# Moving tokens' rows to and from the experts by indirect transfers in place of products with zeros and ones

## The chip, the cores and the metric

The kernel runs on one core of one Trainium2 chip; the chip's other cores run nothing. The metric is device time in microseconds (us) of one execution, from the run's own clock. The core has a TensorE (PE in the profile, its weight loads PEld), a VectorE (DVE), a ScalarE (ACT), a GpSimd (POOL) and a SyncE (SP), each with its own instruction stream, which meet by semaphores, and 16 DMA engines that serve transfers issued by SP and by POOL.

## The reference

Two networks follow one another over the same 256 tokens of width 1,024, in float32, batch 1. The part that changes is the mixture of experts in the first network's second layer:

```python
h = modulate(x, moe_norm, shift, scale)        # rmsnorm(x, w) * (1 + scale) + shift
logits = h @ router                            # 256 x 8
top_val, top_idx = lax.top_k(logits, 2)
weights = softmax(top_val)
gate_e = sum(one_hot(top_idx, 8) * weights)    # 256 x 8, two of eight not zero
out = 0
for e in range(8):
    g, u = split(h @ w_gu[e], 2)               # 1024 x 7168
    out = out + gate_e[..., e] * ((silu(g) * u) @ w_down[e])   # 3584 x 1024
x = x + gate * out
```

Each token needs two of the eight experts. Everything before it (two hybrid and dense blocks, a Mamba-2 mixer) and behind it (the final norm, two more hybrid layers) stays as it is.

## The kernel before, in words

The program is a list of stages; `program` calls each stage's `sync`, `tensor`, `vector`, `scalar` and `gpsimd` in turn, so each engine has one fixed order of instructions. Tokens lie on the 128 partitions in two halves of 128 (`hf`). X holds the running sum, xn the normed tokens.

The stage `experts` routes first. `routed_tensor` and `routed_vector` compute the logits, for each token and expert whether it is among the two best (`sel`), and its place in that expert's list (`pos`, a running count by products with a triangular matrix). An expert takes up to CAP = 128 tokens in a round. If one has more, a flag makes every engine run a second round (`again`) for places 128 to 255; all engines read the flag at the end of the first round (`second`).

Then `round_tensor`, `round_scalar` and `round_vector` go through 8 experts x 42 units (`U`). A unit is half of a 2 MB weight tile: 28 units make the hidden rows (seven groups j; gate and up part p_; two halves of the contraction each), 14 units are the projection down. Products run as three float32r products (high by high, low by high, high by low), so each unit is first split: ScalarE copies its rounded part (`split_hi`, line 139), VectorE subtracts (`split_lo`, line 145), then PE multiplies (`use_tensor`, line 132, 12 products of 128x512). Units have three buffers, so the split of unit n waits until PE has used unit n - 3. ScalarE and VectorE run two units ahead of PE (`AHEAD`): in step n they split unit n and then do what belongs to unit n - 2 (`use_scalar`, `use_vector`): the silu and the product of the hidden rows, the split of the transposed hidden rows. SP streams the weight tiles in the order of use (`pieces`, line 177) into three places of 2 MB; a place comes free when VectorE has split its last unit. The weights are 21 tiles an expert.

How tokens come to an expert (`gather_*`): VectorE builds the table Pe of zeros and ones (128 tokens x 128 places for each half) out of pos and sel. PE transposes it (line 136; VectorE copies it to PT) and forms XG = xn' x Pe, which gives the expert's tokens already transposed: 8 column blocks x 2 halves, in two steps of 16 products. VectorE applies scale and shift, and the split follows into XGh and XGl. `coming` places these six steps behind units 29 to 34 of the expert before, one step a unit; for expert 0 they run inside the routing.

How results come back (`put_*`, `rounded_sum_scalar`, `low_sum_vector`): when expert x is done, VectorE multiplies its rows by the gate of the whole block (`summed_vector`, into Y); during the next expert's first eight units the rows are split into Yh and Yl, PE multiplies PT by both for each half of the tokens and of the columns (8 products of 128x512, behind unit 7), and VectorE adds ps x egate into X (line 153, four instructions). The last expert's put follows at the end of the round.

Before this stage, the `mamba` stage's `gpsimd` issues small loads, then two row loads of 512 KB (`row_load`, eb from ssm_sums), then waits for PE before each further one. In `experts`, `gpsimd` loads the router's weights and the final norm, and nothing more until the next stage.

Of the kernel before, what the change touches and what calls it, by code (L numbers as in the profile page):

```python
# [6 lines left out]
F32 = mybir.dt.float32  # L7
# [4 lines left out]
D = 1024  # L12
T = 256
# [10 lines left out]
NE = 8  # L24
BIG = 1e30
CAP = 128


def constants():

    p = np.arange(128)
    c = {}
    c["ident"] = np.eye(128)
    c["causal"] = p[:, None] <= p[None, :]
    c["glamask"] = (p[:, None] <= p[None, :]) & (p[:, None] // 64 == p[None, :] // 64)
    lev = np.zeros((128, 7, 128))
    for n in range(7):
        b = p >> n
        lev[:, n, :] = (b[None, :] % 2 == 1) & (b[:, None] == b[None, :] - 1)
    c["levels"] = lev.reshape(128, -1)  # L40
    dist = np.zeros((128, 256))
    dist[:, :128] = 128 + p[:, None] - p[None, :]
    dist[:, 128:] = np.where(p[:, None] >= p[None, :], p[:, None] - p[None, :], BIG)
    c["dist"] = dist
    dc = np.full((128, 2, 16), BIG)
    for h in range(2):
        t = h * 128 + p
        for n in range(15):
            dc[:, h, n] = np.where(n * 16 + 31 <= t, t - (n * 16 + 15.5), BIG)
    c["distc"] = dc.reshape(128, -1)  # L50
    c["blockdiag"] = (p[:, None] // 16 == np.arange(8)[None, :])
    c["cmask"] = np.where(p[:, None] >= p[None, :], 0.0, -BIG)
    half = 8
    inv = np.float32(500000.0) ** (-np.arange(half, dtype=np.float32) / np.float32(half))
    ang = np.arange(T, dtype=np.float32)[None, :] * inv.astype(np.float32)[:, None]
    cos, sin = np.ones((128, T)), np.zeros((128, T))
    perm = np.zeros((128, 128))
    for b in (0, 64):
        cos[b:b + 8] = cos[b + 8:b + 16] = np.cos(ang.astype(np.float32))
        sin[b:b + 8] = -np.sin(ang.astype(np.float32))  # L60
        sin[b + 8:b + 16] = np.sin(ang.astype(np.float32))
        for i in range(8):
            perm[b + 8 + i, b + i] = 1
            perm[b + i, b + 8 + i] = 1
    c["cos"], c["sin"], c["perm"] = cos, sin, perm
    e = np.arange(8)
    c["tie"] = np.broadcast_to((e[None, :] < e[:, None]).reshape(1, 64), (128, 64))
    c["iota"] = np.broadcast_to(np.arange(256)[None], (128, 256))
    c["before"] = p[:, None] < p[None, :]
    c["reset64"] = np.broadcast_to((np.arange(T) % 64 != 0)[None], (128, T))  # L70
    c["reset128"] = np.broadcast_to((np.arange(T) % 128 != 0)[None], (128, T))
    return {k: np.ascontiguousarray(v, dtype=np.float32) for k, v in c.items()}
# [42 lines left out]
DONE = Done()  # L115
# [3 lines left out]
class Engine:  # L119
# [56 lines left out]
    def dma_start(self, o, i):  # L176
        return self.e.dma_start(o, i) if self.e else DONE

# [1947 lines left out]
def mamba(c):  # L2126
# [40 lines left out]
    for i in range(16):  # L2167
# [3 lines left out]
        if i % 4 == 3:  # L2171
            k = i // 4
# [29 lines left out]
    sums = c.nc.dram_tensor("ssm_sums", (32, T), F32).ap()  # L2202
    sums_landed, row_landed = c.event_signal("ssm_sums_landed", 16), [c.event_signal(f"ssm_row{i}_landed", 16) for i in range(2)]
# [16 lines left out]
    def gpsimd(e):  # L2220
# [8 lines left out]
        for j in range(2):  # L2229
            row_load(e, j)  # L2230
        for j in range(8):
# [284 lines left out]
def experts(c):  # L2516
# [15 lines left out]
    fl, fli = c.sb("fl", [1, 2], ph), c.sb("fli", [1, 1], ph, mybir.dt.int32)  # L2532
    ph.close()
# [5 lines left out]
    Pe = c.put(68.5, "Pe", [128, 2, 128])  # L2539
    hrow = [c.put(70.5 + 2 * i, f"hrow{i}", [128, 512]) for i in range(2)]  # L2540
# [44 lines left out]

    def gather_tensor(e, S, blk, x, step):
        if step == 1:
# [6 lines left out]
        if step in (2, 3):  # L2594
            k0 = 4 * (step - 2)
            ps = ubanks.take((S.name, "XG", x, k0))
            e.wait_ge(*ps.was)
            e.wait_ge(*S.v.at(("Pe", x)))
# [5 lines left out]
    def gather_vector(e, S, blk, x, step):  # L2604
        if step == 0:
# [5 lines left out]
        if step == 2:  # L2611
            ps = c.psum.of((S.name, "PT", x))
            e.wait_ge(*S.t.at(("PT", x)))
            if x > 1:
                e.wait_ge(*S.t.at(("put", x - 2)))
# [82 lines left out]
    def use_tensor(e, S, W, n):  # L2698
        x, l = at(n)
        hi, lo = W.parts(e, n)  # L2700
        if l < 28:
# [14 lines left out]
            if l == 7 and x:  # L2716
                put_tensor(e, S, x - 1)
# [21 lines left out]
    def use_scalar(e, S, n):  # L2739
        x, l = at(n)  # L2740
        if l == 2 and x:
            rounded_sum_scalar(e, S, x - 1)
# [28 lines left out]
    def use_vector(e, S, n):  # L2771
        x, l = at(n)
        if l == 4 and x:
            low_sum_vector(e, S, x - 1)
        if l < 28:
# [9 lines left out]
            if l == 7 and x:  # L2785
                put_vector(e, S, x - 1)
            return
# [4 lines left out]

    def summed_vector(e, S, x):
        e.wait_ge(*c.side.v.at(("gate", "moe")))
        e.wait_ge(*(S.t.at(("put", x - 1)) if x else M.t.at("logits")))
# [71 lines left out]
    def routed_vector(e):  # L2867
# [21 lines left out]
        e.tensor_reduce(sel[:, :, :].rearrange("p h e -> p (h e)"), e3(p1), ALU.add).then_inc(*v.up())  # L2889
        e.wait_ge(*v.now())  # L2890
        e.tensor_scalar(sel[:, :, :], sel[:, :, :], 1.5, ALU.is_lt).then_inc(*v.up("sel"))
# [8 lines left out]
        e.tensor_scalar(fl[:, 1:2], fl[:, 0:1], CAP + 0.5, ALU.is_gt).then_inc(*v.up())  # L2900
        e.wait_ge(*v.now())
        e.tensor_copy(fli[:, :], fl[:, 1:2]).then_inc(*v.up("flag"))
        e.wait_ge(*M.a.at("L"))
# [6 lines left out]
        e.tensor_tensor(gt[:, :, :], gt[:, :, :], bc(e1_[:, :], 2, 8), ALU.mult).then_inc(*v.up("gate"))  # L2910

# [15 lines left out]
    def gpsimd(e):  # L2927
        before.wait_for(e, "end")
        e.dma_start(rw[:, :, :], io["moe_router"][0].rearrange("(k p) e -> p k e", p=128)).then_inc(*router_landed.up("router"))
        e.dma_start(fn[:, :], io["final_norm"].partition_broadcast(128)).then_inc(*norm_landed.up("norm"))  # L2930
        M.g.mark("end")
# [1145 lines left out]
```

## Time and profile before

| what | us |
|---|---|
| median of three runs | 2509.26 |
| lowest, highest | 2507.23, 2512.62 |
| the profiled execution's own time | 2510.2 |
| its span, first to last instruction | 2508.4 |

| engine | busy us | share of the span |
|---|---|---|
| PE | 2374.4 | 95% |
| PEld | 2078.2 | 83% |
| DVE | 1976.5 | 79% |
| ACT | 1460.8 | 58% |
| POOL | 219.3 | 9% |

Times in the profile count from the span's start. A row of a timeline has the start, the length, the engine, the line of the kernel, the operation and its tiles, and in brackets how long the engine was idle before it and what released it. The line is often that of a helper (132 is every product, 136 every transpose, 145 every two-operand VectorE instruction), so tiles tell the operations apart. An engine that is not on the chain of waits may idle at no cost, and a busy PE is not PE at its peak. A DMA share is the mean busy share of the 16 DMA engines.

### The profile page before, as it was taken

What the parts mean: (1) busy time and instruction counts of PE and PEld (TensorE: products, weight loads), DVE (VectorE), ACT (ScalarE), POOL (GpSimd) and SP (SyncE); (2) the same over time, 40 slices, a digit from 0 to 9 for tenths busy, and PEclk for the clock granted to TensorE, in tenths of its full rate; (3) what the DMA queues carried; (4) which work ended last, traced back from release to release, by engine and by line L of the source; (5) the groups of instructions that cost most, each with busy time, mean ns of one, the idle gap of its engine ahead of it and who ended that gap; (6) DMA issues with size and microseconds to landing.
All of it is one profiled execution on the core that took longest, in us unless ns stands there. A gap on an engine that the chain in (4) does not pass through costs nothing.

```text
span 2508.4 us, 33025 instructions
## 1 busy us (share of the span) xinstructions
PE 2374.4 (95%) x13939; PEld 2078.2 (83%) x13939; DVE 1976.5 (79%) x2135; ACT 1460.8 (58%) x1679; POOL 219.3 (9%) x271
## 2 busy tenths in 40 slices
PE   5898999899989999999999999998999999899998
PEld 4776998798878888888888888887888997887997
DVE  6857876699669989898989998986667865767875
ACT  3334433467557777677777777774555654445562
POOL 1100111101000000000000000001401211320110
PEclk9987998999989999999999999999999999999999
DMA  9753677444459999999999999985124554223551
GB/s 328 245 189 127 251 282 291 176 170 168 172 193 369 343 371 344 363 350 360 355 361 353 361 355 355 361 343 187 68 101 151 200 191 159 98 77 119 209 211 68
DMA packets 143031, 612.71 MB, mean 244 GB/s; under 512 B 18696, under 2 KB 33370, under 8 KB 121370
## 3 DMA queue, kind: packets, MB, share of 16 engines
q1 hardware_dynamic: 125968, 554.39, 59.7%
q0 software_dynamic: 15824, 55.72, 6.4%
q8 instruction: 111, 1.82, 0.3%
q10 hardware_dynamic: 1082, 0.40, 0.1%
q14 instruction: 46, 0.38, 0.0%
HBM read 609.40 MB, written 1.08 MB: 243 GB/s over the span
## 4 chain that ended last, share of the span: by engine, by line
PE 79%; DVE 12%; ACT 4%; DMA 3%; issue 2%; POOL 1%; SPq 0%; DVEq 0%; ACTq 0%; POOLq 0%
PE ps L132 76%; PE ps L136 3%; DVE macc L153 1%; DVE eb L145 1%; DVE gate L153 1%; DVE ul_ssm_w L145 1%; DMA beside<-in_moe_mod_w 1%; DMA slots<-in_hyb_mod_w 1%; ACT xn L139 1%; DMA beside<-in_dense_mod_w 1%; DVE xn L150 0%; DVE xn L153 0%; DVE ul_in L145 0%; POOL Ci L145 0%; DVE xn L145 0%
## 5 line engine op out<-in xcount | busy, mean ns | idle before, releaser
L145 DVE TENSOR_TENSOR ul_moe_w<-slots,uh_moe_w 128x2048 fp32r<-128x2048 f32 x334 | 761.5, 2289 | 90.4 <-ACT uh_moe_w L139 89.4
L139 ACT ACTIVATE uh_moe_w<-slots 128x2048 fp32r<-128x2048 f32 x334 | 640.0, 1917 | 199.8 <-PE ps L132 167.2
L132 PE MATMUL ps<-uh_moe_w,XGh 128*128 128x512 f32 x896 | 354.4, 396 | 3.1 <-DVE XGl L145 2.1
L132 PE MATMUL ps<-uh_moe_w,XGl 128*128 128x512 f32 x896 | 349.6, 390 | 0.0
L132 PE MATMUL ps<-ul_moe_w,XGh 128*128 128x512 f32 x896 | 349.0, 389 | 0.0
L145 DVE TENSOR_TENSOR ul_ffn<-slots,uh_ffn 128x2048 fp32r<-128x2048 f32 x64 | 145.8, 2291 | 79.3 <-ACT uh_ffn L139 79.3
L132 PE MATMUL ps<-HTf,uh_ffn 128*128 128x256 f32 x704 | 199.4, 283 | 2.0 <-DVE HTlf L145 2.0
L132 PEld LDWEIGHTS ps<-uh_moe_w,XGh 128*128 128x128 f32 x896 | 168.3, 188 | 39.8 <-DVE ul_moe_w L145 3.8
L132 PE MATMUL ps<-HTf,ul_ffn 128*128 128x256 f32 x704 | 199.2, 283 | 0.0
L132 PE MATMUL ps<-HTlf,uh_ffn 128*128 128x256 f32 x704 | 199.2, 283 | 0.0
L132 PEld LDWEIGHTS ps<-uh_moe_w,XGl 128*128 128x128 f32 x896 | 168.2, 188 | 35.9
L132 PEld LDWEIGHTS ps<-ul_moe_w,XGh 128*128 128x128 f32 x896 | 168.4, 188 | 33.3
L132 PE MATMUL ps<-uh_moe_w,ehTh 128*128 128x512 f32 x448 | 177.2, 396 | 0.0
L132 PE MATMUL ps<-ul_moe_w,ehTh 128*128 128x512 f32 x448 | 174.6, 390 | 0.0
L139 ACT ACTIVATE uh_ffn<-slots 128x2048 fp32r<-128x2048 f32 x66 | 125.4, 1910 | 72.4 <-PE ps L132 70.7
L132 PE MATMUL ps<-uh_moe_w,ehTl 128*128 128x512 f32 x448 | 138.1, 389 | 0.0
L132 PEld LDWEIGHTS ps<-HTf,uh_ffn 128*128 128x128 f32 x704 | 135.1, 192 | 2.4 <-DVE HTlf L145 2.4
L132 PEld LDWEIGHTS ps<-HTlf,uh_ffn 128*128 128x128 f32 x704 | 135.2, 192 | 0.0
L132 PEld LDWEIGHTS ps<-HTf,ul_ffn 128*128 128x128 f32 x704 | 135.2, 192 | 0.0
L139 ACT ACTIVATE uh_dense_w<-slots 128x2048 fp32r<-128x2048 f32 x33 | 62.9, 1911 | 83.3 <-PE ps L132 83.2
L132 PE MATMUL ps<-HTm,uh_in 128*128 128x256 f32 (+1 forms) x336 | 100.8, 300 | 4.2 <-DVE ul_in L145 3.0
L145 DVE TENSOR_TENSOR ul_dense_w<-slots,uh_dense_w 128x2048 fp32r<-128x2048 f32 x33 | 75.5, 2289 | 36.2 <-ACT uh_dense_w L139 36.0
(530 smaller groups left out, 5531.6 us busy)
## 6 DMA issues: line engine op xcount, KB each, us to landing
slots<-in_moe_w_gu SPq DMA_DIRECT2D x111, 2048.0 KB, 9.4
slots<-in_moe_w_down SPq DMA_DIRECT2D x56, 2048.0 KB, 9.0
slots<-in_w_up SPq DMA_DIRECT2D x20, 2048.0 KB, 8.0
slots<-in_w_in SPq DMA_DIRECT2D x14, 2048.0 KB, 8.7
slots<-in_dense_w_gu SPq DMA_DIRECT2D x10, 2048.0 KB, 11.1
slots<-in_ssm_w_in SPq DMA_DIRECT2D x10, 2048.0 KB, 8.4
slots<-in_w_down SPq DMA_DIRECT2D x10, 2048.0 KB, 8.3
slots<-in_dense_w_down SPq DMA_DIRECT2D x5, 2048.0 KB, 10.9
```

The source lines that it names most:

```text
L132: return self.e.matmul(o, lhsT, rhs, start=start, stop=stop, skip_group_check=skip) if self.e else DONE
L136: return self.e.transpose(o, i, ident[0:n, 0:n]) if self.e else DONE
L139: return self.e.activation(o, i, f, **kw) if self.e else DONE
L145: return self.e.tensor_tensor(o, a, b, op) if self.e else DONE
L153: return self.e.scalar_tensor_tensor(o, a, s, b, op0, op1) if self.e else DONE
```

## The change

Row numbers are worked out in the routing. `place` is a new constant (each expert's first row, and rows out of the way). For each token and each of its two choices, VectorE forms the row place + pos, or a row out of the way (from NOWHERE) if the place is over 127: `to`, and `fro`, the same but at most row 896. 15 small VectorE instructions do this, 12 ahead of the gates and three behind (`share`, the weights of the two choices).

Two tables in memory, `moe_sent` and `moe_made`, take rows of 4 KB. POOL zeroes those parts of them that may be read without having been written, in the mamba stage, by eight stores of 512 KB. After the routing, POOL scatters xn into `moe_sent` by four indirect transfers (two halves x two choices, 128 rows each). For experts 1 to 7 POOL loads the 128 rows of an expert into Xrow, and PE transposes them (eight transposes of 128x128) in place of the 16 products a step; expert 0 keeps its products. The results of experts 0 to 6 are stored from Y to `moe_made` in place of the put. During expert 7, four indirect transfers gather each token's two rows, and VectorE adds them to X, times their share, behind units 12, 14, 16 and 18. Expert 7 keeps its table and its put, and the second round keeps everything.

```diff
+NOWHERE = (NE + 2) * CAP
...
+    c["place"] = np.concatenate([np.tile(np.arange(NE) * CAP, (128, 2)), NOWHERE + p[:, None] + np.array([[0, 128]])], 1)
...
+    def scatter_rows(self, o, rows, i):
+        return self.e.indirect_dma_start(o, bass.IndirectOffsetOnAxis(ap=rows, axis=0), i, None) if self.e else DONE
+
+    def gather_rows(self, o, i, rows):
+        return self.e.indirect_dma_start(o, None, i, bass.IndirectOffsetOnAxis(ap=rows, axis=0)) if self.e else DONE
...
+    zero = c.put(41.5, "zero", [128, 256])
+    c.sent = c.nc.dram_tensor("moe_sent", (NOWHERE + T, D), F32).ap()
+    c.made = c.nc.dram_tensor("moe_made", (NE * CAP, D), F32).ap()
+    c.zeroed = c.event_signal("moe_rows_zeroed", 16)
...
         e.wait_ge(*sums_landed.at("sums"))
         for j in range(2):
             row_load(e, j)
+        e.memset(zero[:, :], 0.0).then_inc(*g.up("zero"))
+        e.wait_ge(*g.at("zero"))
+        for x in range(1, NE):
+            e.dma_start(c.sent[x * CAP:(x + 1) * CAP, :].rearrange("p (a n) -> p a n", n=256), bc(zero[:, :], 1, 4)).then_inc(*c.zeroed.up("zeroed"))
+        e.dma_start(c.made[(NE - 1) * CAP:NE * CAP, :].rearrange("p (a n) -> p a n", n=256), bc(zero[:, :], 1, 4)).then_inc(*c.zeroed.up("zeroed"))
         for j in range(8):
...
+    Xrow, Yrow = c.put(120, "Xrow", [128, D]), [HT[:, 0:4, :].rearrange("p a b -> p (a b)"), c.put(120, "Yrow1", [128, D]), c.put(102.5, "Yrow2", [128, D])]
...
+    def placed(S, x):
+
+        return S is again or x in (0, NE - 1)
...
     def gather_tensor(e, S, blk, x, step):
-        if step == 1:
+        if step == 1 and (S is again or x == NE - 1):
...
             e.wait_ge(*ps.was)
+            if S is M and x:
+                e.wait_ge(*xrow_landed.at(("xrow", x)))
+                for k in range(k0, k0 + 4):
+                    m = e.transpose(ps.t[:, (k - k0) * 128:(k - k0 + 1) * 128], Xrow[:, k * 128:(k + 1) * 128], K["ident"])
+                m.then_inc(*S.t.up(("XG", x, k0)))
+                return
...
-        if step == 0:
+        if step == 0 and placed(S, x):
...
-        if step == 2:
+        if step == 2 and (S is again or x == NE - 1):
             ps = c.psum.of((S.name, "PT", x))
             e.wait_ge(*S.t.at(("PT", x)))
-            if x > 1:
+            if x > 1 and S is again:
...
-            if l == 7 and x:
+            if l == 7 and x and S is again:
                 put_tensor(e, S, x - 1)
...
-        if l == 2 and x:
+        if l == 2 and x and S is again:
             rounded_sum_scalar(e, S, x - 1)
...
-        if l == 4 and x:
+        if l == 4 and x and S is again:
             low_sum_vector(e, S, x - 1)
...
-            if l == 7 and x:
+            if l == 7 and x and S is again:
                 put_vector(e, S, x - 1)
+            if S is M and x == NE - 1 and l in COMING_BACK:
+                come_back_vector(e, COMING_BACK.index(l))
...
+    COMING_BACK = (12, 14, 16, 18)
+
+    def come_back_vector(e, i):
+        o = X[:, i % 2, :]
+        e.wait_ge(*M.v.at("share"))
+        e.wait_ge(*yrow_landed[i % 3].at(("yrow", i)))
+        if i > 1:
+            e.wait_ge(*M.v.at(("back", i - 2)))
+        e.scalar_tensor_tensor(o, Yrow[i % 3][:, :] if i % 3 else Yrow[0], share[:, i:i + 1], o, ALU.mult, ALU.add).then_inc(*M.v.up(("back", i)))
+        if i == 3:
+            M.v.mark(("X", NE - 2))
+
     def summed_vector(e, S, x):
         e.wait_ge(*c.side.v.at(("gate", "moe")))
-        e.wait_ge(*(S.t.at(("put", x - 1)) if x else M.t.at("logits")))
+        if x and S is M:
+            e.wait_ge(*made_landed.at(("made", x - 1)))
+        else:
+            e.wait_ge(*(S.t.at(("put", x - 1)) if x else M.t.at("logits")))
...
+        e.tensor_reduce(rank[:, :, :].rearrange("p h e -> p (h e)"), e3(p1), ALU.add).then_inc(*v.up("rank"))
         e.wait_ge(*v.now())
-        e.tensor_scalar(sel[:, :, :], sel[:, :, :], 1.5, ALU.is_lt).then_inc(*v.up("sel"))
+        e.tensor_scalar(sel[:, :, :], rank[:, :, :], 1.5, ALU.is_lt).then_inc(*v.up("sel"))
...
         e.tensor_scalar(fl[:, 1:2], fl[:, 0:1], CAP + 0.5, ALU.is_gt).then_inc(*v.up())
+        e.tensor_scalar(one[:, :, :], rank[:, :, :], 0.5, ALU.is_lt).then_inc(*v.up())
+        e.wait_ge(*place_landed.at("place"))
+        for hf in range(2):
+            e.tensor_scalar(over[:, hf, :], pos[:, hf, :], CAP - 0.5, ALU.is_gt, place[:, 16 + hf:17 + hf], ALU.mult).then_inc(*v.up())
+        e.tensor_tensor(row[:, :, :].rearrange("p h e -> p (h e)"), pos[:, :, :].rearrange("p h e -> p (h e)"), place[:, 0:16], ALU.add).then_inc(*v.up())
         e.wait_ge(*v.now())
         e.tensor_copy(fli[:, :], fl[:, 1:2]).then_inc(*v.up("flag"))
+        e.tensor_tensor(sec[:, :, :], sel[:, :, :], one[:, :, :], ALU.subtract).then_inc(*v.up())
+        e.tensor_tensor(row[:, :, :], row[:, :, :], over[:, :, :], ALU.max).then_inc(*v.up())
+        e.wait_ge(*v.now())
+        for i, w in enumerate((one, sec)):
+            e.tensor_tensor(pick[:, 2 * i:2 * i + 2, :], row[:, :, :], w[:, :, :], ALU.mult).then_inc(*v.up())
+        e.wait_ge(*v.now())
+        e.tensor_reduce(rowf[:, :], pick[:, :, :], ALU.add).then_inc(*v.up())
+        e.wait_ge(*v.now())
+        e.tensor_copy(to[:, :], rowf[:, :]).then_inc(*v.up("to"))
+        e.tensor_scalar(rowm[:, :], rowf[:, :], float((NE - 1) * CAP), ALU.min).then_inc(*v.up())
+        e.wait_ge(*v.now())
+        e.tensor_copy(fro[:, :], rowm[:, :]).then_inc(*v.up("fro"))
...
         e.tensor_tensor(gt[:, :, :], gt[:, :, :], bc(e1_[:, :], 2, 8), ALU.mult).then_inc(*v.up("gate"))
+        e.wait_ge(*v.now())
+        for i, w in enumerate((one, sec)):
+            e.tensor_tensor(pick[:, 2 * i:2 * i + 2, :], gt[:, :, :], w[:, :, :], ALU.mult).then_inc(*v.up())
+        e.wait_ge(*v.now())
+        e.tensor_reduce(share[:, :], pick[:, :, :], ALU.add).then_inc(*v.up("share"))
...
         e.dma_start(fn[:, :], io["final_norm"].partition_broadcast(128)).then_inc(*norm_landed.up("norm"))
+        e.dma_start(place[:, :], c.cn["place"]).then_inc(*place_landed.up("place"))
+        e.wait_ge(*c.zeroed.at("zeroed"))
+        e.wait_ge(*M.v.at("to"))
+        for i in range(4):
+            e.scatter_rows(c.sent[:, :], to[:, i:i + 1], xn[:, i % 2, :]).then_inc(*sent_landed.up("sent"))
+        e.wait_ge(*sent_landed.at("sent"))
+
+        def fetch(x):
+            if x > 1:
+                e.wait_ge(*M.t.at(("XG", x - 1, 4)))
+            e.dma_start(Xrow[:, :], c.sent[x * CAP:(x + 1) * CAP, :]).then_inc(*xrow_landed.up(("xrow", x)))
+
+        fetch(1)
+        for x in range(NE - 1):
+            if x + 2 < NE:
+                fetch(x + 2)
+            e.wait_ge(*M.v.at(("Y", x, 1)))
+            e.dma_start(c.made[x * CAP:(x + 1) * CAP, :], Y).then_inc(*made_landed.up(("made", x)))
+        e.wait_ge(*made_landed.at(("made", NE - 2)))
+        e.wait_ge(*M.v.at("fro"))
+        e.wait_ge(*M.v.at(("XGl", NE - 1, 4)))
+        e.wait_ge(*M.t.at(("XG", NE - 1, 4)))
+        for i in range(4):
+            if i > 2:
+                e.wait_ge(*M.v.at(("back", i - 3)))
+            e.gather_rows(Yrow[i % 3][:, :] if i % 3 else Yrow[0], c.made[:, :], fro[:, i:i + 1]).then_inc(*yrow_landed[i % 3].up(("yrow", i)))
         M.g.mark("end")
         again.g.mark("end")
```

## Rows read from the trace of the kernel before

**Rows 1.** The page's part 2, GB/s moved in each of 40 slices of the span

```profile
GB/s 328 245 189 127 251 282 291 176 170 168 172 193 369 343 371 344 363 350 360 355 361 353 361 355 355 361 343 187 68 101 151 200 191 159 98 77 119 209 211 68
```

**Rows 2.** Table by stretch (us from the span's start), the stage before and the experts

```profile
core 0: us, PE busy (x) PEld busy (x) DVE busy (x) ACT busy (x) POOL busy (x), PEclk, DMA share, GB/s
520.00:560.00 40.00, 36.88 (x304) 35.03 (x303) 38.52 (x66) 27.55 (x38) 3.98 (x5) 1.00 0.43 155
717.00:760.00 43.00, 41.99 (x191) 34.38 (x190) 36.74 (x28) 31.99 (x22) 0.00 (x0) 1.00 0.64 239
760.00:800.00 40.00, 40.00 (x184) 33.06 (x183) 36.54 (x22) 30.48 (x22) 0.00 (x0) 1.00 0.99 375
1080.00:1200.00 120.00, 119.99 (x559) 99.22 (x559) 109.72 (x77) 86.68 (x59) 0.00 (x0) 1.00 0.93 354
1560.00:1680.00 120.00, 120.00 (x544) 99.27 (x543) 109.44 (x71) 89.43 (x61) 0.00 (x0) 1.00 0.94 358
```

**Rows 3.** Waits in 720 to 1700: who, for whom, us, times, longest

```profile
ACT uh_moe_w L139 <- PE ps L132: 167.2, 217, 2.7
...
ACT uh_moe_w L139 <- DMA slots<-in_moe_w_gu: 28.8, 27, 1.9
```

**Rows 4.** Chain that ended last, 690 to 1780: start, length, what

```profile
800.52 5.49 PE ps L132 x24
...
1666.11 35.20 PE ps L132 x155
```

**Rows 5.** DMA issues by line: count, KB each, median us to landing

```profile
slots<-in_moe_w_gu SPq DMA_DIRECT2D x111, 2048.0 KB, 9.4
...
out<-X SPq DMA_DIRECT2D x2, 512.0 KB, 2.6
```

**Rows 6.** PE in order of time, 800 to 816: start, length, operation

```profile
799.92 0.60 PE L136 MATMUL ps<-k_ident,hrow 128*128 128x128 f32 x4
800.28 0.48 PE L132 MATMUL ps<-uh_moe_w,ehTh 128*128 128x512 f32 x1
...
808.89 1.95 PE L132 MATMUL ps<-Pe,xn 128*128 128x128 f32 x16
810.59 0.48 PE L132 MATMUL ps<-uh_moe_w,ehTh 128*128 128x512 f32 x1
```

**Rows 7.** PE in order of time, 862 to 872, the put and what follows

```profile
862.39 0.39 PE L132 MATMUL ps<-eYh,PTe 128*128 128x512 f32 x1
...
864.21 0.39 PE L132 MATMUL ps<-uh_moe_w,XGh 128*128 128x512 f32 x1
```

**Rows 8.** Instructions on tile eb: duration ns min/median/max, first and last start

```profile
L177 POOL DMA_DIRECT2D eb<-ssm_sums x8: 763/792/1177, 495.9 to 614.5; - x8
...
DMA to landing us min/median/max: 4.1/5.6/9.6
```

**Rows 9.** VectorE in order of time, 1530 to 1720, the last expert

```profile
1583.56 1.28 DVE L145 TENSOR_TENSOR HT<-ps,gate 128x512 f32<-128x512 f32 x2
...
1625.85 4.58 DVE L145 TENSOR_TENSOR ul_moe_w<-slots,uh_moe_w 128x2048 fp32r<-128x2048 f32 x2 [0.75 <-ACT uh_moe_w L139]
...
1633.57 2.29 DVE L145 TENSOR_TENSOR ul_moe_w<-slots,uh_moe_w 128x2048 fp32r<-128x2048 f32 x1 [0.34 <-ACT uh_moe_w L139]
...
1711.77 1.28 DVE L153 SCALAR_TENSOR_TENSOR X<-X,rst,gate 128x1024 f32<-128x1024 f32 x1 [5.04 <-ACT rst L139]
```

**Rows 10.** VectorE in order of time, 697 to 765, the stage's start

```profile
717.33 0.15 DVE L159 TENSOR_REDUCE fl<-ps 1x1 f32<-1x8 f32 x1
...
718.53 2.29 DVE L145 TENSOR_TENSOR ul_moe_w<-slots,uh_moe_w 128x2048 fp32r<-128x2048 f32 x1
```

**Rows 11.** PE in order of time, 700 to 860, the stage's start

```profile
708.75 0.69 PE L136 MATMUL ps<-k_ident,Pe 128*128 128x128 f32 x2 [0.91 <-DVE Pe L150]
709.23 5.40 PE L132 MATMUL ps<-Pe,xn 128*128 128x128 f32 x32
...
722.27 0.39 PE L132 MATMUL ps<-uh_moe_w,XGh 128*128 128x512 f32 x1
```

More of the change, by code:

```diff
@@ L2532, in experts @@
     fl, fli = c.sb("fl", [1, 2], ph), c.sb("fli", [1, 1], ph, mybir.dt.int32)
+    place = c.sb("place", [128, 18], ph)
+    rank, one, sec, row, over = [c.sb(n, [128, 2, NE], ph) for n in ("erank", "eone", "esec", "erow", "eover")]
+    pick, share = c.sb("epick", [128, 4, NE], ph), c.sb("eshare", [128, 4], ph)
+    rowf, rowm = c.sb("erowf", [128, 4], ph), c.sb("erowm", [128, 4], ph)
+    to, fro = c.sb("eto", [128, 4], ph, mybir.dt.int32), c.sb("efro", [128, 4], ph, mybir.dt.int32)
     ph.close()
@@ L2539, in experts @@
     Pe = c.put(68.5, "Pe", [128, 2, 128])
+    Xrow, Yrow = c.put(120, "Xrow", [128, D]), [HT[:, 0:4, :].rearrange("p a b -> p (a b)"), c.put(120, "Yrow1", [128, D]), c.put(102.5, "Yrow2", [128, D])]
+    place_landed, sent_landed = c.event_signal("place_landed", 16), c.event_signal("moe_sent_landed", 16)
+    xrow_landed, made_landed = c.event_signal("moe_xrow_landed", 16), c.event_signal("moe_made_landed", 16)
+    yrow_landed = [c.event_signal(f"moe_yrow{i}_landed", 16) for i in range(3)]
     hrow = [c.put(70.5 + 2 * i, f"hrow{i}", [128, 512]) for i in range(2)]
@@ L2888, in routed_vector @@
         e.wait_ge(*v.now())
-        e.tensor_reduce(sel[:, :, :].rearrange("p h e -> p (h e)"), e3(p1), ALU.add).then_inc(*v.up())
+        e.tensor_reduce(rank[:, :, :].rearrange("p h e -> p (h e)"), e3(p1), ALU.add).then_inc(*v.up("rank"))
         e.wait_ge(*v.now())
-        e.tensor_scalar(sel[:, :, :], sel[:, :, :], 1.5, ALU.is_lt).then_inc(*v.up("sel"))
+        e.tensor_scalar(sel[:, :, :], rank[:, :, :], 1.5, ALU.is_lt).then_inc(*v.up("sel"))
         ps = c.psum.of("moe_pos")
```

## The prediction

> **What bounds the kernel now.** I read the page first, for where the experts lie: of its 40 slices of 62.7 us, number 13 to 27 (752 to 1693 us) move 343 to 371 GB/s, almost twice what the slices before and after them move [rows 1]. Second view, the table by stretch: from 760 us on PE is busy for the whole of each stretch at a granted clock of 1.00 (the 2.4 GHz level), while the DMA engines stand at 0.93 to 0.99 and POOL does nothing [rows 2]. The reader is to see two resources full at once. Third, who waits: ScalarE's weight split waits 167.2 us for PE and 28.8 us for weights that have not landed [rows 3]. So PE sets the pace, and the weight stream follows close behind. Fourth, the chain of waits, which repeats by expert: the same piece stands at 800.52 and, seven experts on, at 1666.11 [rows 4]. 865.59 us / 7 = **123.66 us a cycle**, and each cycle holds one gather and one put.
>
> What the stream needs: a cycle loads 21 weight tiles of 2,048 KB [rows 5], 21 x 2.097 = 44.04 MB, in 123.66 us 356 GB/s. The best 40 us stretch moved 375 at a share of 0.99 [rows 2]; at a share of 1 that would be 379.
>
> **What goes from PE.** The gather of one expert is two steps of 16 products with zeros and ones. The first begins at 808.89 and the next weight product at 810.59, so 1.70 us a step. Four transposes of 128x128 (the hidden rows' own, of the form that the change puts in their place) take 799.92 to 800.28, 0.36 us [rows 6]. Two steps give 2 x (1.70 - 0.36) = 2.68. The two transposes of the table that go are half of such a group, 0.18. The put is eight products from 862.39 to 864.21, 1.82 us [rows 7]. Together **4.68 us a cycle**, so PE alone could go at 118.98. VectorE and ScalarE lose work too; neither is the bound, so it counts for nothing.
>
> **What comes to the DMA engines.** In each cycle one load of the next expert's rows and one store of a result, 512 KB each: 1.05 MB, so 45.09 MB. A store of that size landed after 2.6 us [rows 5], a POOL load after 5.6 in the median [rows 8]; both have most of a cycle of cover, so only their bytes count. At 375 GB/s a cycle takes 45.09 / 0.375 = **120.24 us**, at 379 it takes 118.97, just PE's pace. I take 375, which a stretch of 40 us really delivered, rather than a rate worked out from its share: the stream becomes the bound by a little. Six cycles gain 6 x 3.42 = 20.5 us.
>
> The Trainium skill (HBM Reference, section Specifications) puts the effective bandwidth per core at about 358 GB/s, and has a core that streams alone well above it. The trace disagrees with the first figure as a ceiling: 375 GB/s [rows 2]. By 358 a cycle would be an estimated 126 us and the change a loss.
>
> **The last cycle** has no further row load and four gathers of 512 KB (2.10 MB) in its place: 44.04 + 0.52 + 2.10 = 46.66 MB, 124.4 us against 123.66: +0.7. In the same stretch VectorE adds four scaled rows into X. An instruction of that shape took 1.28 us; four are 5.12. VectorE is idle 0.75 and 0.34 us in four units of weights, 2.2 in the eight over which the additions are spread [rows 9], so it falls 2.9 us behind, and PE with it: 118.98 + 2.9 = 121.9, under the 124.4 and so hidden by the stream. Ends: 0, or 5.1 if nothing covers it.
>
> Do the rows come back in time? Expert 6's result is ready at 1583.56 + 1.28 = 1584.8 [rows 9]; its store must land, then three gathers follow. Indirect transfers have no row. The nearest are POOL's loads of 512 KB: 0.79 us to issue, 4.1 to 9.6 to landing [rows 8]. With 9.6 for each, the first lands at about 1606. VectorE wants it at unit 12, about 1622; the fourth is issued after the first addition, 1623, and wanted six units later, about 1639, so it has 16 us. I take no wait. Behind one, if it comes, stands VectorE's next low-part subtraction, and so PE.
>
> **The start.** VectorE gets 15 small instructions for the row numbers ahead of the low part of unit 2. The seven there now take 717.33 to 718.53, 0.17 each [rows 10], so 2.6 us. The table's transposes went, so everything begins at 708.75 instead of 709.23, 0.48 earlier [rows 11]. Unit 2's low part, now from 718.53 and 2.29 long, then ends at 720.82 - 0.48 + 2.57 = 722.9; PE wants it at 722.27 - 0.48 = 721.8. Stall 1.1, less 0.5: **+0.6**, with ends of -0.5 (absorbed) and +3 (all 15 on the path). The other engines read the overflow flag only at the stage's end. On POOL's queue come, behind two loads of constants, the table of places (one small load, wanted 25 us later), the wait for the row numbers, four scatters and the first row load; nothing else is queued there until the next stage. Scatters and load are 2.62 MB, 7.0 us at 375 GB/s, and from 717 to 760 the DMA share is 0.64, so 15 us are free [rows 2]. At 0.8 + 9.6 us each, one after the other, all five are done 52 us after 721, by 774; PE wants the rows at 809. Counted at nothing; without that cover 7.
>
> **The zeroing**, in the stage before: eight stores of 512 KB are 8 x 0.79 = 6.3 us of POOL and 4.19 MB, 11 us of DMA. In 520 to 560 POOL is busy 3.98 us of 40 and the DMA share is 0.43 [rows 2], which hides both. Counted at 0; the end is 3, if weights there land late.
>
> **Sum:** -20.5 + 0.7 + 0.6 = -19.2 us. The profiled execution took 2510.2 us (span 2508.4, 1.8 around it); the median of the three runs is 2509.26, 0.9 less. 2509.3 - 19.2 gives **2490 us**. At 379 GB/s six cycles gain 28.1, the last 0.5: 2481. At 370, about halfway to the rate of no gain below, a cycle is 121.9 and the last 126.1: -10.6 + 2.4 + 0.6, 2502. So this case spans 2481 to 2502.
>
> **Rivals.** *PE keeps the pace.* The stream delivers more than 379; then all 7 x 4.68 = 32.8 us come, less 0.6 and the 2.9 of VectorE's additions: 2480 us. For it: the share of 0.99 was no stop for PE, which was busy throughout. Against: weights are waited for already [rows 3].
>
> *The stream is the wall, and the kernel gets slower.* Place: the DMA engines, in every expert. It decides at 45.09 / 123.66 = 365 GB/s: if stores and row loads among the weights hold the sum to what long stretches show now (354 and 358 over 120 us [rows 2]), a cycle at 358 is 125.9; six lose 13.7, the last, 46.66 / 0.358 = 130.3, loses 6.7, and with 0.6 for the start it is 2530 us. For it: those are the rates of whole cycles. Against: PE set them, since no tile comes free while it gathers and puts; where it only multiplied, the stream gave 375. Close to 365 the six cycles are a draw, and the last and the start cost 4.2 + 0.6: 2514.
>
> *The rows come back late.* It decides where the fourth gather takes over 16 us from issue to landing. At 25, 9 us of VectorE's wait become PE's, and gathers two and three may add as much again: 10 to 15 us, so 2500 to 2505. For it: 128 rows picked by number, put into queues by POOL, against a full stream. Against: POOL is otherwise idle, and its loads took at most 9.6 [rows 8].
>
> **Chances.** Forecast 0.55, PE keeps the pace 0.2, late rows 0.1, slower stream 0.15. A measurement of this kernel can tell about 0.2%, 5 us, from no change. Faster by more than that: nearly all of the first two and a third of the late rows, 0.75; within it: the rest of the late rows and the edge of the slower stream, 0.12; slower 0.13. The range runs from just under PE's pace, 2478, to 2512; it leaves out the slower stream.
>
> **What would show it.** Forecast: cycles of 120 to 121 us, a DMA share of 0.97 or more throughout, ScalarE waiting more than 28.8 us for weights and less for PE. First rival: cycles of 119 with no more waits for weights. Second: cycles over 123.7 with long waits for weights. Third: a VectorE wait for returned rows between 1600 and 1640. A gap of about 1 us in PE at the stage's third unit bears out the start. I am wrong in the mechanism if cycles stay over 121 us without waits for weights, or if time comes or goes outside 700 to 1710 us.

## Result, and the profile after the change

The changed kernel takes 2492.02 us (median of four runs, 2488.02 to 2493.95) against 2510.94 for the kernel before beside it (2507.23 to 2514.14): ratio 0.9923, 95% interval 0.9904 to 0.9943. The profiled execution took 2491.49 us, its span is 2489.7. In five more runs of the unchanged file it was 0.9912 (0.9897 to 0.9926). By the medians 19 and 23 us are gained; 2490 was forecast. The total hides two errors of opposite sign, and a pace whose cause was another than the one named.

The page. Its GB/s line by slice answers to [rows 1], the others to its parts 1 and 3:

```profile
PE 2343.0 (94%) x13701; PEld 2046.0 (82%) x13701; DVE 1950.8 (78%) x2093; ACT 1454.8 (58%) x1665; POOL 249.2 (10%) x303
...
GB/s 321 238 209 133 248 261 307 154 248 171 173 208 370 383 372 387 374 386 374 372 369 386 372 383 361 400 294 179 83 96 144 203 203 153 102 68 126 210 206 68
...
HBM read 615.18 MB, written 11.04 MB: 252 GB/s over the span
```

Slices 13 to 25 moved 343 to 371 GB/s before and 361 to 387 now: a shorter cycle, with two more transfers in it. The helpers stand two lines lower in the changed kernel: 134 is every product, 138 every transpose, 141 ScalarE's copies, 147 every two-operand VectorE instruction.

The table by stretch (answers to [rows 2]) and the waits from 720 to 1690 us (answer to [rows 3]), of the changed kernel:

```profile
core 0: us, PE busy (x) PEld busy (x) DVE busy (x) ACT busy (x) POOL busy (x), PEclk, DMA share, GB/s
840.00:880.00 40.00, 40.00 (x183) 32.87 (x182) 36.80 (x22) 29.79 (x20) 0.54 (x1) 1.00 0.98 393
880.00:920.00 40.00, 40.00 (x183) 33.09 (x182) 35.96 (x22) 31.11 (x23) 0.00 (x0) 1.00 0.98 378
960.00:1000.00 40.00, 40.00 (x183) 33.09 (x183) 36.77 (x23) 29.90 (x21) 0.54 (x1) 1.00 0.98 395
```

```profile
ACT uh_moe_w L141 <- PE ps L134: 121.3, 194, 1.5
...
ACT uh_moe_w L141 <- DMA slots<-in_moe_w_gu: 46.3, 44, 2.9
...
PEld ps L134 <- DVE ul_moe_w L147: 14.7, 26, 1.4
```

The reader is to see two things. A share of 0.98 goes with 378 GB/s and with 395: the share does not say how far the rate is from its end. And ScalarE waits less for PE (121.3 against 167.2) and more for weights (46.3 against 28.8), as the forecast had asked for; the experiments show that this sign fits another cause as well.

For the length of a cycle I take the first product with hidden rows of an expert, PE in order of time. Of experts 0, 6 and 7, first in the kernel before, then in the changed one:

```profile
797.20 0.39 PE L132 MATMUL ps<-uh_moe_w,ehTh 128*128 128x512 f32 x1
...
1539.36 0.39 PE L132 MATMUL ps<-uh_moe_w,ehTh 128*128 128x512 f32 x1
...
1662.78 0.39 PE L132 MATMUL ps<-uh_moe_w,ehTh 128*128 128x512 f32 x1
```

```profile
799.60 0.39 PE L134 MATMUL ps<-uh_moe_w,ehTh 128*128 128x512 f32 x1
...
1517.46 0.39 PE L134 MATMUL ps<-uh_moe_w,ehTh 128*128 128x512 f32 x1
...
1640.15 0.39 PE L134 MATMUL ps<-uh_moe_w,ehTh 128*128 128x512 f32 x1
```

The first six cycles: (1539.36 - 797.20) / 6 = 123.69 before, (1517.46 - 799.60) / 6 = **119.64** after. The last: 123.42 before, **122.69** after.

The chain that ended last, around the gather of expert 2 and of expert 4, in the changed kernel (start, length, what):

```profile
922.20 8.23 PE ps L134 x36
...
930.51 1.93 ACT uh_moe_w L141
...
932.50 2.17 issue
934.67 1.36 DVE HT L152 x4
936.03 2.20 DVE ul_moe_w L147
938.23 1.28 DVE HT L152 x4
939.52 2.20 DVE ul_moe_w L147
941.72 1.21 DVE XGl L147 x2
942.92 2.21 DVE ul_moe_w L147
...
945.18 30.21 PE ps L134 x132
...
1181.12 2.21 DVE ul_moe_w L147
1183.35 10.58 DMA slots<-in_moe_w_gu
1193.95 1.93 ACT uh_moe_w L141
1195.90 2.30 DVE ul_moe_w L147
```

(`issue` is the chain's name for time in which an engine waits for nothing that the profile shows. At 932.50 it is no idle time: in order of time VectorE works from 932.46 to 934.75 on the low part of a unit.) Before, this chain was PE alone in every cycle, of which [rows 4] has two pieces. Now each cycle has a stretch of some 15 us in which VectorE is the late one: two scalings of the gathered block, the block's low parts and the low parts of three units stand in its queue while PE spends 0.35 us on four transposes (930.26 to 930.61 us) where it spent 1.70 on products [rows 6]. In some cycles, as in expert 4's, the lateness goes on: a tile's place comes free late, the next tile lands in it 10.58 us later, and PE waits for that. These are the longer cycles (119.3, 119.1, 119.1, 120.8, 119.1, 120.4).

From the start of the span to its end the 18.7 us between the two profiled spans are: +1.47 ahead of the stage that holds the zeroing, +0.07 in it, +0.85 at the start of the experts, -24.30 in six cycles, -0.73 in the last, +0.04 to the end of the round, +3.72 from there to the next stage's queries (52.61 us before, 56.33 after), +0.17 in the rest.

### The profile page after: what moved, and what is told of

It is laid out like the page before. It is cut to its first block, busy times and chain, and to the rows that moved or that the text cites. A ratio compares the mean times of both kernels' runs of the same rounds, so it can differ in the third digit from the quotient of the medians.

```text
span 2489.7 us, 32549 instructions
## 1 busy us (share of the span) xinstructions
PE 2343.0 (94%) x13701; PEld 2046.0 (82%) x13701; DVE 1950.8 (78%) x2093; ACT 1454.8 (58%) x1665; POOL 249.2 (10%) x303
## 4 chain that ended last, share of the span: by engine, by line
PE 70%; DVE 17%; DMA 5%; ACT 5%; issue 3%; POOL 1%; SPq 0%; DVEq 0%; ACTq 0%; POOLq 0%
PE ps L134 67%; DVE ul_moe_w L147 3%; PE ps L138 2%; DMA slots<-in_moe_w_gu 2%; DVE macc L155 1%; ACT uh_moe_w L141 1%; DVE eb L147 1%; DVE gate L155 1%; DMA beside<-in_moe_mod_w 1%; DVE ul_ssm_w L147 1%; DMA slots<-in_hyb_mod_w 1%; DVE HT L152 1%; ACT xn L141 1%; DMA beside<-in_dense_mod_w 1%; DVE xn L155 0%
## 5 line engine op out<-in xcount | busy, mean ns | idle before, releaser
L141 ACT ACTIVATE uh_moe_w<-slots 128x2048 fp32r<-128x2048 f32 x334 | 639.3, 1918 | 181.2 <-PE ps L134 121.3
```

What stands on the lines that cost most here:

```text
L141: return self.e.activation(o, i, f, **kw) if self.e else DONE
```

## The experiments

Cycle lengths of all kernels, in us, measured as above, with the time of each run (single runs, but for the first two rows and the last two, which are medians):

| kernel | mean of six cycles | last cycle | time |
|---|---|---|---|
| before | 123.69 | 123.42 | 2510.94 |
| changed | 119.64 | 122.69 | 2492.02 |
| more2 | 120.45 | 123.03 | 2491.79 |
| more4 (without its first cycle) | 121.45 | 123.76 | 2522.69 |
| less | 119.48 | 122.29 | 2482.76 |
| gather_only | 122.08 | 122.28 | 2501.66 |
| gather_act | 121.05 | 120.84 | 2496.71 |
| put_only | 122.06 | 125.19 | 2504.53 |
| small_gathers | 119.67 | 120.75 | 2487.91 |
| small_adds | 119.62 | 120.88 | 2479.96 |
| act_scale | 119.61 | 122.15 | 2486.91 |
| less_act | 119.37 | 122.13 | 2497.56 |
| best | 119.10 | 121.35 | 2489.23 |
| after_again | 119.93 | 122.65 | 2489.01 |

The times of single runs say little: the stage before the experts begins between 449.2 and 458.8 us over these kernels, although the code ahead of it is the same in all. The cycles are what is compared.

**Is the stream the bound? more2, more4, less.** In more2 (nine in place of five in more4):

```diff
-            e.dma_start(Xrow[:, :], c.sent[x * CAP:(x + 1) * CAP, :]).then_inc(*xrow_landed.up(("xrow", x)))
+            for r in range(5):
+                if r:
+                    e.wait_ge(*xrow_landed.now())
+                e.dma_start(Xrow[:, :], c.sent[x * CAP:(x + 1) * CAP, :]).then_inc(*xrow_landed.up(("xrow", x)))
```

Expected of more2:

> Each expert's rows are loaded five times instead of once, into the same tile, one load after the other: 4 x 0.524 = 2.10 MB more in a cycle of one expert (47.19 MB), six times, and nothing else. Theory A (the stream is the bound, as the prediction had it, at the 378.6 GB/s that the first cycles after the change moved): the first six cycles take 47.19 / 0.3786 = 124.6 us, 5.0 more than the 119.64 of the changed kernel, and the whole kernel about 2522. Theory B (PE's pace of 118.98 sets the cycle and the stream could carry more, up to the 393 to 395 GB/s of its best 40 us): 47.19 / 0.394 = 119.8 us a cycle, the whole within 3 us of 2492. In between the cycle itself measures the rate at which the stream is full: 47.19 MB over its length.

Measured: 120.45 a cycle, where a stream that is full at 378.6 GB/s needs 124.6. Expected of more4, written once this was known:

> Each expert's rows are loaded nine times instead of once, one load after the other: 8 x 0.524 = 4.19 MB more in each of the first six cycles (49.28 MB). Four extra loads (2.10 MB) lengthened the six cycles by 0.81 us each (119.64 to 120.45), and the stream then moved 391 GB/s over 840 us. Theory B (PE's pace with a reserve in the stream that reaches to about 400 GB/s): the wall is met now, 49.28 / 0.400 = 123.2 us a cycle; a loss that merely grows in step with the added loads, 0.4 us for each 1.05 MB, gives 121.3 instead and the wall is still further off (406 GB/s). Theory A (wall at 378.6) would give 130 and is already out.

Measured: the first cycle took 137.0 us, since the nine loads of expert 1's rows were not done when PE wanted them (its one wait of 13.9 us for them); the five cycles after it 121.45. Table by stretch (columns as above), over the middle cycles of the changed kernel, of more2 and of more4:

```profile
918.00:1517.00 599.00, 596.33 (x2703) 490.32 (x2702) 541.67 (x342) 442.27 (x292) 5.33 (x10) 1.00 0.97 377
```

```profile
917.00:1518.00 601.00, 597.12 (x2700) 489.02 (x2699) 539.66 (x340) 441.45 (x290) 15.88 (x30) 1.00 0.99 393
```

```profile
941.00:1548.00 607.00, 600.05 (x2700) 487.75 (x2699) 539.36 (x341) 441.56 (x290) 26.46 (x50) 1.00 0.99 406
```

The stream carried 406 GB/s for 607 us with PE busy for 98.9% of them. So 378.6 (45.09 MB in the 119.1 us of the four short cycles) was what PE's pace asked for, and the bound was not there. More bytes still cost a little: 0.81 us for 2.10 MB and 1.81 for 4.19, or 0.52 and 1.52 against the second profile of the changed kernel, which comes last in this section (119.93). Their DMA issues by line give the median landing of a gate or up tile in the same stretches as 9.7, 10.2 and 10.5 us, and where a tile's place came free late, PE waits for that landing.

The other direction, less: no row loads after expert 1's, no stores but expert 6's.

```diff
-                e.wait_ge(*xrow_landed.at(("xrow", x)))
+                e.wait_ge(*xrow_landed.at(("xrow", 1)))
...
-            if x + 2 < NE:
-                fetch(x + 2)
...
+            if x == NE - 2:
...
```

> The rows of expert 1 serve experts 2 to 7's place and are loaded once, and only expert 6's result is stored: this leaves out the other experts' own rows and the return of results 0 to 5, and takes 1.05 MB from each of the middle cycles (44.04 MB left), with PE's work as in the changed kernel. Theory A (stream the bound at 378.6 GB/s): cycles fall to PE's pace, 118.98, or a little under the 119.64 measured, and every cycle is the same; gain in the six cycles about 4 us. Theory B (PE's pace with a small reserve): the four cycles at 119.1 stay where they are, the two longer ones (120.8 and 120.4) lose their waits for weights, 3 us in all. Common to both: ScalarE's waits for weights fall from 58.9 us toward the 32.5 of the kernel before. If cycles stay at 119.6 with waits for weights, the added bytes were not what made weights late.

Measured: 119.48. ScalarE's waits for gate and up weights fell from 46.3 to 35.4 us, and the cycle by 0.16 (0.45 against the second profile). So the added bytes are at most a part of what keeps a cycle over PE's 118.98; a difference of 0.16 is smaller than that between two profiles of one kernel.

**The two halves alone.** In gather_only the results come back by products again (every test for the first round taken out, the stores, gathers and additions too); in put_only the rows go out by products:

```diff
-            if x > 1 and S is again:
+            if x > 1:
...
-            if l == 7 and x and S is again:
+            if l == 7 and x:
...
```

```diff
-            if S is M and x:
+            if False:
...
-        fetch(1)
...
```

> Rows go out by transfers and transposes, results come back by products with the table, as before. By the prediction's sum of PE's work a cycle is 123.66 - 2.68 = 120.98 us if PE sets the pace (theory B), and the kernel before's 123.66 less 2.68 is well over what 44.57 MB need at 378.6 GB/s (117.7), so both theories say 121.0; what is tested is the size of the gather term. If transposes cost more than 0.36 us for four, or VectorE's three instructions behind each step hold PE up, it is over 121.5. The last cycle has the put in place of the four returning gathers and should be like the others.

> Rows go out by products with the table, as before; results are stored and fetched back by row number. By the prediction's sum a cycle is 123.66 - 1.82 - 0.18 = 121.66 us if PE sets the pace, and the stream (44.57 MB, 117.7 us at 378.6 GB/s) does not bind, by either theory. If the put's removal is worth more than its eight products (the low and high parts on VectorE and ScalarE, which go with it), the cycle is under 121.4. The last cycle has the four gathers and additions: 2 to 4 us longer than the others by theory A (bytes) and by B (VectorE's additions).

Measured: 122.08 and 122.06. Both are over the sums, gather_only by 1.10, put_only by 0.40, which is near the scatter found below and was not followed up. And the last cycle behaves as it should if the return costs it something: it is 3.13 over the mean in put_only, which has the return, and 0.20 in gather_only, which has not. For the 1.10 the suspect was VectorE, so gather_act moves one of the two scalings of each block to ScalarE, in gather_only:

```diff
+        if step == 4 and S is M and x:
...
+            for k in range(4, 8):
+                e.activation(XGf[:, k, :], ps.t[:, (k - 4) * 128:(k - 3) * 128], AF.Identity, scale=s1[:, k:k + 1], bias=s2[:, k:k + 1]).then_inc(*S.a.up(("XGf", x, 4)))
```

> Rows go out by transfers and transposes, results come back by products, and the scaling of each block's second half is on ScalarE. With the scaling on VectorE the six cycles took 122.08 us against 120.98 by the sum of PE's work. If VectorE, which here still has the put's low parts and sums, is what holds PE up where the gather's products used to give it time, cycles fall to 121.0 to 121.4. If they stay over 121.8, the gather's saving is lost elsewhere: the sum of PE's work was wrong, or weights land late.

Measured: 121.05 against 120.98 by the sum. The chain from 800 to 1530 us by line, first gather_only, then gather_act:

```profile
by line: PE ps L134 77.2%; DVE ul_moe_w L147 7.0%; DMA slots<-in_moe_w_gu 5.6%; PE ps L138 2.7%; ACT uh_moe_w L141 2.6%; DVE HT L152 2.2%; issue 1.6%; DVE XGl L147 1.0%; ACTq L131 0.0%
```

```profile
by line: PE ps L134 89.7%; PE ps L138 3.4%; DMA slots<-in_moe_w_gu 2.7%; DVE ul_moe_w L147 1.9%; ACT uh_moe_w L141 1.6%; ACT HT L141 0.4%; DVE XGl L147 0.3%; issue 0.1%; DVEq L131 0.0%
```

Moving 1.28 us of VectorE's work was worth 1.03 us a cycle, and with it went half of the chain's waits for weights, though not a byte less was moved. That shows how weights come late here: VectorE's subtraction frees a tile's place late.

**The same relief in the full change: act_scale, less_act.** act_scale is that edit on the changed kernel, less_act has it on less.

> The scaling of the second half of each gathered block (four instructions, 1.28 us together on VectorE) goes to ScalarE, for experts 1 to 7; nothing else changes. Theory B (what is left over PE's 118.98 in a cycle, 0.66 us, is VectorE falling behind where the gather stands, after which the three weight tiles come free late): cycles fall to 119.0 to 119.3, and the pieces of the chain on VectorE and on weight loads behind the gather get fewer. Theory A (bytes): cycles stay at 119.6. If ScalarE becomes the late one there, cycles rise over 119.8 with ScalarE on the chain at the gather.

> Both reliefs at once: no row loads and stores in the middle cycles (this leaves out, as before, experts 2 to 7's own rows and the return of results 0 to 5) and the scaling of every block's second half on ScalarE. Each alone left the six cycles where they were (119.48 and 119.61 against 119.64), although the shortest cycle fell to 118.64 with the second. If two limits of nearly the same size stand behind each other (VectorE where the gather stands, the weights' landing behind it), both together give 118.7 to 119.0 and nearly no weight wait on the chain. If the cycles stay at 119.5, what is left over PE's pace comes from neither.

Measured: 119.61 and 119.37, no gain that the scatter would show. The chain of act_scale shows where the time goes now. At the gather of expert 2 it is PE throughout, and then:

```profile
928.90 21.85 PE ps L134 x96
...
950.77 1.93 ACT uh_moe_w L141
...
952.72 0.57 DVE ul_moe_w L147
953.29 1.64 issue
954.93 1.28 DVE HT L147 x2
956.21 4.41 DVE ul_moe_w L147 x2
...
960.64 11.48 DMA slots<-in_moe_w_gu
```

The next late place is 24 us on, where VectorE scales the expert's finished result. Here too `issue` is no wait; VectorE in order of time has no pause at that place:

```profile
952.72 2.29 DVE L147 TENSOR_TENSOR ul_moe_w<-slots,uh_moe_w 128x2048 fp32r<-128x2048 f32 x1 [0.37 <-ACT uh_moe_w L141]
954.93 1.28 DVE L147 TENSOR_TENSOR HT<-ps,gate 128x512 f32<-128x512 f32 x2
956.13 4.48 DVE L147 TENSOR_TENSOR ul_moe_w<-slots,uh_moe_w 128x2048 fp32r<-128x2048 f32 x2
```

The two scalings (1.28 us) stand between low parts, so the two low parts behind them end only at 960.61, and the tile that takes the place they free lands 11.48 us after that. The changed kernel has the same piece in one cycle in its chain (1437.04 to 1456.20). So one lateness stood behind the other, and relieving the first showed the second. This is read from the chain; no run moved these scalings. That the lateness had more cover in gather_act, where the put gives VectorE 1.82 us of PE's time, is likely but not shown, and what each is worth in the full change wasn't separated further.

**The last cycle: small_gathers, small_adds.** First the edit of small_gathers (its additions also read xn in place of Yrow), then that of small_adds:

```diff
-            e.gather_rows(Yrow[i % 3][:, :] if i % 3 else Yrow[0], c.made[:, :], fro[:, i:i + 1]).then_inc(*yrow_landed[i % 3].up(("yrow", i)))
+            e.dma_start(Yrow[0][:, 64 * i:64 * i + 64], c.made[0:128, 64 * i:64 * i + 64]).then_inc(*yrow_landed[i % 3].up(("yrow", i)))
```

```diff
-        e.scalar_tensor_tensor(o, Yrow[i % 3][:, :] if i % 3 else Yrow[0], share[:, i:i + 1], o, ALU.mult, ALU.add).then_inc(*M.v.up(("back", i)))
+        e.scalar_tensor_tensor(o[:, 0:64], (Yrow[i % 3][:, :] if i % 3 else Yrow[0])[:, 0:64], share[:, i:i + 1], o[:, 0:64], ALU.mult, ALU.add).then_inc(*M.v.up(("back", i)))
```

> The four gathers of results become four plain loads of 64 columns (32 KB each) and the additions read other rows of the same size, so VectorE's work stays: this leaves out the return of the results. It takes 2.0 MB from the last cycle, which is 122.69 us in the changed kernel, 3.05 over its mean cycle of 119.64. Theory A (the last cycle is set by its bytes): it falls by 2.0 / 0.379 = 5.3 us or to PE's pace, about 119.5. Theory B (VectorE's four additions of 1.28 us set it, the transfers are covered): it stays within 0.7 us of 122.7.

> The four gathers stay, the four additions work on 64 of 1,024 columns: this leaves out most of the return of the results and takes about 4.8 us of VectorE's work from the last cycle. Theory A (bytes): the last cycle stays at 122 to 123 us. Theory B (VectorE's additions): it falls to the level of the others, 119.5 to 120.

Measured: 120.75 and 120.88, against 122.69. Each takes away about 1.9 of the 3.05 us that the last cycle has over the others. Neither theory had it alone: in the changed kernel late weights (two landings of 10.75 and 12.21 us on the chain, beside the gathers) and then VectorE's additions stand one after the other on the same chain. From 1570 us to the end of that cycle, the chain of small_gathers has no landing and that of small_adds no addition.

**A version that might beat both, and the scatter: best, after_again.** best has the scaling on ScalarE, the additions behind units 12, 17, 22 and 27, and the arithmetic for rows, gates and flag out of the start, in seven portions that stand in `later`:

```diff
-    COMING_BACK = (12, 14, 16, 18)
+    COMING_BACK = (12, 17, 22, 27)
...
+            if S is M and x == 0 and 8 <= l < 8 + len(later):
+                later[l - 8](e, M.v)
...
```

> Three moves: the arithmetic for row numbers, gates and flag leaves the start of the stage and is spread over units 8 to 14 of expert 0; the four additions stand behind units 12, 17, 22 and 27 of the last expert instead of 12, 14, 16 and 18; and the second half of each block is scaled by ScalarE. By theory B: the start gives back the 0.85 us it cost (from the first rounding of the gathered rows to the first product of hidden rows, 82.92 us before and 83.77 after the change), the last cycle falls from 122.69 to 120.9, where it stood without the additions' columns, and the six cycles stay at 119.6; together 2.5 to 3 us, about 2489 in the median against 2492. If the last cycle is still over 122, additions that late hold up something else, the gathers or the put of the last expert.

> The changed kernel once more, unaltered, as the measure of scatter. The runs so far gave six-cycle means of 119.64 (changed), 119.48 (fewer bytes), 119.61 (scaling on ScalarE), 119.37 (both), 119.10 (scaling on ScalarE, additions and start spread). Theory B says that single waits for weights of 1 to 1.6 us fall on some cycles and not on others, so that one profile of the same kernel may differ from the next by some tenths of a microsecond a cycle: a second profile between 119.2 and 119.9 would make all differences under 0.4 us scatter. If it comes at 119.64 within 0.1, the 0.5 us of the last of those kernels is an effect. The time in the median is expected at 2492, within 2 us.

Measured: best 0.9914 (0.9901 to 0.9928), the changed kernel again 0.9912 (0.9897 to 0.9926), each against the kernel before in the same call: no difference. The second profile of the changed kernel has cycles of 119.93, 0.3 from the first; so less, act_scale and less_act are within that difference of the first profile or near it, and best's 119.10 lies below both, with a last cycle of 121.35 instead of 122.65. Two profiles are a thin measure of scatter, and best has one. But best's start did not get shorter (84.61 us from ScalarE's first rounding of gathered rows to the first product with hidden rows, 83.77 in the changed kernel, 82.92 before), and it lost 1.4 to 1.7 us more than the changed kernel behind the stage (58.03 against 56.33 and 56.66).

## Why the prediction was right in its total, and which steps failed

**PE's saving of 4.68 us a cycle: right, if anything too small.** Four cycles of the changed kernel take 119.09 to 119.28, where PE alone was put at 118.98; single cycles of act_scale, less_act and best go down to 118.58, so PE alone needs some tenths less than the sum said. gather_act gives the gather's 2.68 within 0.07.

**"VectorE and ScalarE lose work too; neither is the bound, so it counts for nothing": wrong for VectorE.** That VectorE lost work was the smaller matter; it lost the time that PE's products had given it. PE's 1.35 us less in each gather step made VectorE the late one for some 15 us of every cycle, and cost 1.1 us of the 2.68 where the gather was changed alone. VectorE's busy share, 91% of the cycles before and 90% after, did not show it; its order in that stretch did.

**"At 375 GB/s a cycle takes 120.24 us: the stream becomes the bound by a little": the step that failed.** The cycle came out near it, 119.64 and 119.93, for another reason, and just under the forecast's sign of 120 to 121; its two other signs came (a share of 0.97 over the middle cycles, more waits for weights and fewer for PE), but fit the other cause as well. 375 GB/s at a share of 0.99 [rows 2] was read as the stream's end; it was what PE took. The stream gave 406 at the same share. In place of a rate that binds, the runs showed places that come free late behind VectorE and then the landing of one tile. The Trainium skill (HBM Reference, section Specifications) puts a core that streams alone at about 425 GB/s; the 406 here agree with it better than the 358 that the prediction weighed.

**The rivals.** "PE keeps the pace" was nearest in the mechanism: its 119 held in four cycles of six. Its sign, no more waits for weights, did not hold, nor its 2480 us. "The stream is the wall" is out by more2 and more4. "The rows come back late" did not happen: no wait of VectorE for returned rows is in the trace. POOL in order of time shows how near it was:

```profile
1561.02 0.54 POOL L179 DMA_DIRECT2D moe_made<-HT  x1 [120.22 <-DVE HT L147]
1574.18 1.34 POOL L185 DMA_INDIRECT HT<-moe_made,efro  x1 [12.62 <-DMA moe_made<-HT]
1575.82 1.87 POOL L185 DMA_INDIRECT Yrow<-moe_made,efro  x1 [0.30 <-issue]
1577.99 2.94 POOL L185 DMA_INDIRECT Yrow<-moe_made,efro  x1 [0.30 <-issue]
1599.30 2.75 POOL L185 DMA_INDIRECT HT<-moe_made,efro  x1 [18.38 <-DVE X L155]
```

POOL waited 12.6 us for the store, and the gathers landed 11.5 to 20.0 after their issue, over the bound of 9.6 taken from plain loads; the fourth, issued at 1599.30, landed after 11.6, by 1610.9, and was added at 1616.46. 5 us of cover were left.

**The last cycle, +0.7 forecast, -0.73 measured.** Its 46.66 MB did not set it, and "hidden by the stream" was wrong for VectorE's additions: taking them away is worth 1.8 us, taking the gathers away 1.9. For the additions alone 2.9 had been worked out, 1.1 too much.

**The start, +0.6 forecast, +0.85 measured.** VectorE's low part begins 3.21 us after the flag's sum (718.99 to 722.20) where it took 1.20 [rows 10]: 2.01 for the 15 instructions, 2.57 forecast. PE's gap at the third unit is 0.46 us (1.1 forecast). Without the table's transposes the routing's last part, from the first product with sel to ScalarE's first rounding of gathered rows, takes 8.43 us instead of 8.74: 0.31, where 0.5 was forecast, and outside the 0.85. **The zeroing, 0 forecast: right within the scatter.** From its stage's start to that first product with sel it was 249.58 us before, 249.97 after and 249.22 in the second profile.

**The sum.** -20.5 + 0.7 + 0.6 was forecast for the experts; -24.30 - 0.73 + 0.85 = -24.2 came. What brought the total back was outside it: +1.47 ahead of all changed code, which is scatter, and +3.72 behind the stage, which was in no term. So it is luck that the total came within 2 us of the forecast, and the prediction's own sign of a wrong mechanism, time that comes or goes outside 700 to 1710 us, applies to the 3.72. There PE stops a second time in its first products:

```profile
1688.86 1.84 PE ps L134 x7
1690.69 1.96 issue
1692.65 2.93 PE ps L134 x13
```

In the kernel before, these 20 products are one piece of 4.61 us. The stop, 1.4 to 3.8 us, stands in eleven of the fourteen profiles, and not in those of before, gather_only and put_only; PE waits in it for nothing that the profile shows. Its cause is open and wasn't tried. The rest goes with the granted clock, 0.91 in 15 us of the next stage (the 2.4 GHz level in the main), 1.00 before. That comes and goes by itself: in the same 15 us it is 1.00 in more2 and less, which have the stop, and 0.90 in put_only, which has not.

## What to carry to other kernels

A DMA share near 1 beside a busy PE is no measure of what the stream can carry: load something twice before a rate is called the end. When work goes from the engine that sets the pace, go through the queue of the next engine at that very place, in order; its share over the stage hides that it was living on the time now removed. And with few buffers, a late release shows as a wait for a transfer: look in the chain at what stands just before the landing, and look up a piece called `issue` in order of time, since it can be the engine's own work.

## What was not expected of the hardware

- 406 GB/s into one core for 607 us at a granted clock of 1.00, at a DMA share of 0.99, the share that stood beside 375 GB/s before.
- Gathers by row number: 128 rows of 4 KB took POOL 1.3 to 2.9 us to issue, where a plain load of 512 KB took it 0.79 in the median [rows 8], and landed after 11.5 to 20.0 us beside the weights, where those plain loads took 4.1 to 9.6.
